# When ACT requests the third and fourth piece of x: all four at the start, or two of them between its roundings

## What is computed

```python
def first_block(x, mem, g_mix, g_mem, w_in, ...):
    h = rms_norm(x, g_mix)
    proj = h @ w_in
    c_h, c_b, c_c, sq, sk, sv, xq, gate_pre = split(proj)
    y_conv = (c_b * causal_depthwise_conv(c_c * c_h, conv_w)) @ w_conv_out
    y_sb   = stick_breaking_attention(sq, sk, sv) @ w_sb_out
    y_x    = memory_cross_attention(xq, rms_norm(mem, g_mem), ...) @ w_x_out
    x = x + (g0 * y_conv + g1 * y_sb + g2 * y_x) @ w_out
    return x + square(relu(rms_norm(x, g_mlp) @ w_up)) @ w_down

def reference(...):
    x = first_block(...)
    for layer in range(2):
        x = hybrid_layer(x, ...)
    return x
```

## Time and profile before

| | |
|---|---|
| time, median of 3 runs | 1200.26 us (1199.26 to 1200.85) |
| the profiled execution | 1199.02 us |
| its span, first to last instruction | 1197.1 us |
| PE busy in the span | 1187.9 us |
| ACT busy | 617.1 us |
| mean granted TensorE clock | 0.998 |

### The profile page before, as it was taken

The page is one execution under the profiler, slowest core; times in us unless marked ns, Lnnn a source line. Parts: engine busy times, 40 slices in busy tenths (PEclk is TensorE's granted clock), DMA queues, the critical chain, the costliest instruction groups (busy, mean ns, idle before and its releaser), DMA issues.

```text
span 1197.1 us, 16485 instructions
## 1 busy us (share of the span) xinstructions
PE 1187.9 (99%) x6484; PEld 1013.6 (85%) x6484; DVE 802.8 (67%) x957; ACT 617.1 (52%) x772; POOL 0.2 (0%) x4
## 2 busy tenths in 40 slices
PE   9999999999999999999999999999999999999997
PEld 7999988888888888888898888888888888888886
DVE  6687976563656676656369697665676878766556
ACT  6577675564444555344256545443436654544441
POOL 0000000000000000000000000000000000000000
PEclk9999999999999999999999999999999999999999
DMA  8555344544555365555364446555536544564550
GB/s 289 204 189 176 141 177 157 203 168 141 224 200 187 119 232 202 185 200 185 106 246 177 150 177 216 207 195 190 188 129 246 174 152 176 195 226 176 196 191 36
DMA packets 35322, 219.25 MB, mean 183 GB/s; under 512 B 4144, under 2 KB 6208, under 8 KB 10176
## 3 DMA queue, kind: packets, MB, share of 16 engines
q1 hardware_dynamic: 34176, 217.37, 50.8%
q10 hardware_dynamic: 1088, 1.05, 0.3%
HBM read 217.34 MB, written 1.06 MB: 182 GB/s over the span
## 4 chain that ended last, share of the span: by engine, by line
PE 96%; DMA 2%; DVE 1%; ACT 1%; issue 0%; SPq 0%; DVEq 0%; ACTq 0%
PE gps L1595 13%; PE gps L1558 12%; PE gps L1613 11%; PE gps L1615 10%; PE gps L1622 10%; PE aps L1615 8%; PE aps L1613 8%; PE aps L1622 8%; PE gps L1599 7%; DMA raw<-w 2%; PE gps L1827 1%; DVE w_lo L877 1%; PE aps L1640 1%; ACT w_hi L386 1%; PE aps L1797 1%; PE aps L1821 1%
## 5 line engine op out<-in xcount | busy, mean ns | idle before, releaser
L877 DVE TENSOR_TENSOR w_lo<-raw,w_hi 128x2048 fp32r<-128x2048 f32 x193 | 441.8, 2290 | 234.2 <-ACT w_hi L386 233.6
L386 ACT ACTIVATE w_hi<-raw 128x2048 fp32r<-128x2048 f32 x193 | 369.6, 1915 | 215.2 <-PE aps L1622 103.1
L1595 PE MATMUL gps<-R_both,w_hi 128*128 128x512 f32 x672 | 167.9, 392 | 0.0
L1613 PE MATMUL aps<-w_hi,Q_hi 128*128 128x512 f32 x416 | 162.2, 390 | 0.0
L1615 PE MATMUL aps<-w_lo,Q_hi 128*128 128x512 f32 x416 | 162.2, 390 | 0.0
L1595 PEld LDWEIGHTS gps<-R_both,w_hi 128*128 128x128 f32 x672 | 122.2, 189 | 22.7
L1613 PE MATMUL gps<-w_hi,H_hi 128*128 128x512 f32 x288 | 114.8, 399 | 0.0
L1615 PE MATMUL gps<-w_lo,H_hi 128*128 128x512 f32 x288 | 112.4, 390 | 0.0
L1622 PE MATMUL aps<-w_hi,Q_lo 128*128 128x512 f32 x416 | 111.5, 390 | 0.0
L1558 PE MATMUL gps<-H_hi,w_hi 128*128 128x256 f32 x416 | 110.0, 287 | 0.7 <-issue 0.7
L1558 PE MATMUL gps<-H_hi,w_lo 128*128 128x256 f32 x416 | 108.4, 283 | 0.0
(11 more groups left out here) (256 smaller groups left out, 1557.8 us busy)
## 6 DMA issues: line engine op xcount, KB each, us to landing
raw<-w SPq DMA_DIRECT2D x192, 1024.0 KB, 4.8
raw<-w SPq DMA_DIRECT2D x16, 256.0 KB, 6.0
B<-rows SPq DMA_DIRECT2D x4, 1024.0 KB, 4.9
B<-turns SPq DMA_DIRECT2D x4, 512.0 KB, 4.6
B<-x_t ACTq DMA_DIRECT2D x4, 256.0 KB, 5.5
B<-mem_t SPq DMA_DIRECT2D x1, 1024.0 KB, 7.5
B<-x SPq DMA_DIRECT2D x1, 1024.0 KB, 6.8
out<-B SPq DMA_DIRECT2D x4, 256.0 KB, 2.1
```

The source lines that it names most:

```text
L386: act.activation(w_hi[:, ring(l), :], raw[:, raw_slot(l), :], ACT.Copy)\
L877: dve.tensor_tensor(w_lo[:, ring(l), :], raw[:, raw_slot(l), :], w_hi[:, ring(l), :].bitcast(F32), ALU.subtract)\
L1595: pe.matmul(b, w_hi[:, r, c:c + P], R_both[:, k, :, :].rearrange("p i t -> p (i t)"), start=(k == 0), stop=False, skip_group_check=True)
L1613: pe.matmul(out, x, w_hi[:, r, c], start=(start and k == ks[0]), stop=False, skip_group_check=resumed)
```

## The change

ACT requests x0 and x1 at the start as before. x2 is requested behind its rounding of w0 and x3 behind its rounding of w1.

```diff
-            for k in range(0, KT, 2):
+            def load_x(k):
                 act.dma_start(B6[:, k:k + 2, :], x_t[k * P:(k + 2) * P].rearrange("(k p) t -> p k t", p=P))\
                    .then_inc(x_piece[k // 2], 16)
+
+            load_x(0)
+            load_x(2)
             act.preload_act_table_set("natural_log_exp_and_others")
             def front_piece(k):
...
             for k in range(KT):
                 front_piece(k)
+                if k < 2:
+                    load_x(4 + 2 * k)
```

## The result

The changed kernel is slower: 1201.95 us median of 20 runs (1200.96 to 1204.88) against 1199.95 us (1199.26 to 1201.46), ratio 1.0018 with a 95% interval of 1.0013 to 1.0024. That is 2.0 us, outside the range of the prediction, and it is the rival to which the prediction gave 0.04.

The account below looks back on a forecast made before the run. PE was taken to bound the kernel, busy 1187.9 of 1197.1 us. w2's landing -0.15, w1 -0.05, handovers +0.05 and the rest 0 gave -0.15 us, so 1200.1 us; range 1199.0 to 1201.5.

Parts of the forecast that it names:

- x2 lands between 8.7 and 10.7: x2's landing after its request at about 5.6 us, from x0's 3.1 and x1's 5.1 us; cost to PE: nothing.
- the two queues' pieces land in turns: Start of the kernel: pieces of ACT's and SP's queues land alternately, x0, w0, x1, w1, x2, w2; no size of its own.
- x2 comes too late: Rival, PE's fifth k: x2 lands behind cst at 13.5, +2.8 us, 1203.0; chance 0.04, of which 0.03 beyond 2.4 us.
- point of decision: x2's landing at 10.7 us, from which on PE's fifth k loses time one for one.
- ACT's requests: Requests moved into ACT's first two roundings: taken as 0, with 0.05 us for two handovers.
- they take ACT's time: Rival, ACT behind its first roundings: requests delay PE's third k by 0.6 to 1.45 us, 1200.9 to 1201.7; chance 0.16.
- they don't move: Rival, ACT's queue: x2 is requested at about 3.9, x3 at about 4.4, time stays 1200.26; chance 0.10.
- w1 sooner: w1's landing at the start: it gains 0 to 0.2 us, taken as -0.05 us.
- the change does more for the weights: Rival, start of the kernel: w1 lands at 6.3 to 6.5, -0.5 to -0.9 us, 1199.4 to 1199.8; chance 0.10.
- w2 sooner: w2's landing before PE's third k: about 7.8 instead of 8.6, of which 0.15 us is used, -0.15 us.
- The count of packets: Queues at 5.2 us: 7 packets of x2 begun, 41 of w1 left, 169 more needed for w2.

Follow-up runs that it names:

- x_by_sp: Against the changed kernel, SP requests x2 between w3 and w4 and x3 between w5 and w6, ACT only x0 and x1; 1200.02 us, ratio 0.9997.
- one_later: Against the changed kernel, x2 is requested behind the rounding of w1 and x3 behind that of w2, one place later; 1204.05 us, ratio 1.0034.
- one_later_warm: Against one_later, six multiplications of zeros are put ahead of PE's fifth k; 1202.72 us, ratio 1.0024.

## Why the prediction was wrong

- *The step that failed* is "x2 lands between 8.7 and 10.7", on which its cost of nothing rested. It landed at 13.8, and PE waited 2.17 us for it. The prediction took the time to landing from x0 and x1 as a property of a queue that is empty or has one piece ahead. Those two were also the first requests of all, with next to nothing in line on either queue. At 5.8 us SP had requested eight pieces of weights and had begun on cst, and of all pieces only x0 and w0 had landed. The right row was the one of the last pieces in line: cst's 7.6 us, and x2 took 8.0.
- *The reading behind it*, "the two queues' pieces land in turns", was true of the landings and wrong as a rule. The requests were made in turns as well, one of ACT and one of SP every half microsecond, so that the rows of before could not tell turns between queues from one line in order of request. (They spoke as little against the rival, where the prediction used them again.) The changed kernel is the first in which they differ, and the packets of ACT's queue stand still for 3.7 us in it. The page of the Trainium skill that the prediction leaned on ("DMA: Bandwidth & Descriptors", "Queues, rings and completion order") has each engine take turns packet by packet. The trace shows that only once x2's packets had begun at all, from 10 us on. By turns from the request on, x2's 0.262 MB at half of 355 GB/s would take 1.5 us, and with the 3.1 us that x0 took in all it would land by 10.4, before the fifth scaling was due (an estimate). The measurement decides on the time. Whether the engines did not take turns, or x2's packets had not yet reached them while earlier requests were being written out, no run here separates.
- *The rival "x2 comes too late"* had the place and the price, and the mechanism in the main: landing behind cst at 13.5 (measured 13.8, beside cst and not behind it), PE's fifth k at 14.7 (14.89), +2.8 us (2.9 in the span, 2.0 in the medians, so that its time of 1203.0 was 1 us too high). Its chance of 0.04 was the error. Its point of decision, a landing at 10.7, came out later in the changed kernel's trace: PE was ready for its fifth k at 14.89 - 2.17 = 12.72 and starts it 1.10 us after the landing, so it felt one from 11.6 on.
- *ACT's requests*: 0 with a bound of 0.6 to 1.45 us. Right: 0.37 us inside the rounding, scaling 0.53 us after it as before. The rows 5.80 and 7.59 refute both the rival that they take ACT's time and the one that they don't move.
- *w1 sooner*, a term of -0.05 us, and the rival that the change does more for the weights: the sign was wrong. w1 was rounded at 7.58 and not before 6.99, and w0 at 5.80 and not 5.57.
- *w2 sooner*: it landed at 8.2, where the prediction had 7.8 and before 8.6. It was rounded at 9.04, since w1 was late; from w1's rounding to w2's it was 1.46 us instead of 1.61, so the 0.15 us were there. They drowned in the wait for x2 two k later.
- *The count of packets* was off: each request counts 16 small packets besides its data. So at 5.2 us x1 was not yet all begun (519 of 544) and none of x2, w1 lacked 432 - 343 = 89 packets and not 41, and w2 576 - 343 = 233 and not 169. It changed no term of the sum.

## What to carry to other kernels

Moving a request back need not shift its landing by as much only: here it went behind nearly all that had been requested in the meantime, on the other queue too. Before a request is delayed, sum what stands in line at its new time, and read its landing from the last transfer of such a line, not from the first ones of the program. To give some transfers precedence, put the others at their place in the order of requests, as x_by_sp does, and not at a later time. x_by_sp takes the loss back; a gain over the kernel before is not shown for it.

## What was unexpected of the hardware

A request on an empty queue did not overtake the backlog of another one: 8.0 us to landing for ACT's, 6.7 us for POOL's, against 3.1 us for the first piece of the program. In these two traces it passed only the transfer requested just before it, cst, by 0.2 and 0.5 us. When ACT made its own, x0, x1, w0 to w7, par and cst had been requested, 10 x 0.262 + 0.02 + 0.33 = 2.97 MB, and the packets begun until 5.8 us held 0.50 and 0.51 MB on the two queues, so some 2.0 MB stood before it; at the 355 GB/s of the earlier trace rows that is 5.5 of the 8.0 us (an estimate). And 2.7 us without work on PE were followed by about 3.4 us at half the clock in one_later's trace, while in the changed kernel's, with 2.2 us idle, the clock stayed at 1.0; with six multiplications of zeros in the gap it stayed at 1.0 in one_later_warm's trace, and the median was 1.3 us lower.
